# Conditioning panels multiplied in fp32 on four 32-column groups, and four of them at the end of the dense layer

## The reference

```python
def adaln(cond, w, b):
    m = jnp.matmul(jax.nn.silu(cond), w) + b
    return jnp.split(m, 3, axis=-1)

def modulated_norm(x, g, shift, scale):
    return rms_norm_2(x, g) * (1 + scale) + shift
```

## Time and profile before

| what | value |
|---|---|
| median of three runs | 2424.51 us |
| the profiled execution's own time | 2424.6 us |
| its span | 2422.5 us |
| TensorE busy in the span | 2317.7 us (96%) |
| VectorE busy | 1770.3 us (73%) |
| ScalarE busy | 1387.8 us (57%) |
| panel loads | 496 of 1024 KB |
| conditioning panels | 24, from 249.7 to 549.7 us |

### The profile page before, as it was taken

How to read it: one execution, slowest core, us unless ns; L and a number is a source line. 1 busy time by engine, 2 the same in 40 slices (tenths; PEclk the granted TensorE clock), 3 DMA queues, 4 the chain that set the end, 5 groups by cost and what they waited for, 6 DMA issues and landing times. The chain is left out here.

```text
span 2422.5 us, 34387 instructions
## 1 busy us (share of the span) xinstructions
PE 2317.7 (96%) x13625; PEld 2002.4 (83%) x13639; DVE 1770.3 (73%) x1687; ACT 1387.8 (57%) x1382; POOL 20.2 (1%) x42
## 2 busy tenths in 40 slices
PE   7998999999998899999999999999989999899998
PEld 7898999999888788888888888888866885778887
DVE  6765655658764689888988898889877667546773
ACT  6464545447463577777777777777764322744442
POOL 0000000000000000000000000000001000000010
PEclk9999999999999899999999999999999999999999
DMA  6233566654333399989998999899980220025400
GB/s 258 105 140 141 202 249 239 248 207 176 105 140 123 141 373 359 375 333 374 358 375 341 367 366 366 341 368 364 367 336 35 78 97 18 1 71 113 113 1 18
DMA packets 81797, 531.80 MB, mean 220 GB/s; under 512 B 16935, under 2 KB 17224, under 8 KB 17480
## 3 DMA queue, kind: packets, MB, share of 16 engines
q1 hardware_dynamic: 81528, 528.95, 58.8%
q10 hardware_dynamic: 144, 1.05, 0.1%
HBM read 528.91 MB, written 1.05 MB: 219 GB/s over the span
## 5 line engine op out<-in xcount | busy, mean ns | idle before, releaser
L2389 DVE TENSOR_TENSOR ring_low<-ring,M_high 128x2048 fp32r<-128x2048 f32 x336 | 760.9, 2289 | 105.7 <-ACT M_high L1356 99.1
L1356 ACT ACTIVATE M_high<-ring 128x2048 fp32r<-128x2048 f32 x336 | 633.2, 1911 | 4.6 <-DMA ring<-panels 4.0
L485 PE MATMUL ps<-M_high,xe_parts 128*128 128x512 f32 x1344 | 449.2, 397 | 0.0
L485 PEld LDWEIGHTS ps<-M_high,xe_parts 128*128 128x128 f32 x1344 | 252.7, 188 | 51.8
L485 PE MATMUL ps<-ring_low,xe_parts 128*128 128x512 f32 x672 | 262.2, 390 | 0.0
L2261 DVE TENSOR_TENSOR W_low<-ring,W_high 128x2048 fp32r<-128x2048 f32 x66 | 150.2, 2291 | 108.4 <-ACT W_high L1356 108.4
L485 PE MATMUL ps<-h_parts,ring_low 128*128 128x256 f32 x704 | 201.3, 286 | 0.0
L485 PE MATMUL ps<-h_parts,B_high 128*128 128x256 f32 x1024 | 188.6, 286 | 3.6 <-DVE ring_low L2040 1.9
L1356 ACT ACTIVATE W_high<-ring 128x2048 fp32r<-128x2048 f32 x66 | 124.9, 1909 | 97.3 <-PE ps L485 97.3
L485 PE MATMUL ps<-M_high,hid_high 128*128 128x512 f32 x448 | 175.9, 393 | 2.1 <-DVE hid_low L2395 2.1
L485 PE MATMUL ps<-M_high,hid_low 128*128 128x512 f32 x448 | 174.4, 389 | 0.0
(11 more groups left out here) (302 smaller groups left out, 4818.5 us busy)
## 6 DMA issues: line engine op xcount, KB each, us to landing
ring<-panels SPq DMA_DIRECT2D x496, 1024.0 KB, 4.8
arena<-rpb SPq DMA_DIRECT2D x32, 64.0 KB, 8.4
cst<-consts SPq DMA_DIRECT2D x1, 1632.0 KB, 11.9
xT<-x SPq DMA_DIRECT2D x1, 1024.0 KB, 4.9
cT<-ctx SPq DMA_DIRECT2D x1, 1024.0 KB, 7.8
arena<-dft SPq DMA_DIRECT2D x1, 1024.0 KB, 14.4
y<-xT ACTq DMA_DIRECT2D x1, 1024.0 KB, 5.8
proj<-w SPq DMA_DIRECT2D x1, 512.0 KB, 6.1
```

What stands on the lines that cost most here:

```text
L485: return nc.tensor.matmul(o, w, m, start=start, stop=stop, skip_group_check=skip)
L1356: return nc.scalar.activation(o, i, fn, **kw)
L2389: V.tensor_tensor(wide_low(q, 0, PW), ring[:, (q % RING) * PW:(q % RING + 1) * PW], moe_high(q, 0, PW).bitcast(F32), ALU.subtract).then_in ...
```

## The change

Conditioning panels are no longer split. TensorE multiplies them in fp32 straight from the ring: the eight row blocks go in turn to four groups of 32 columns of the array, so that blocks k and k + 4 add up in partitions 32 (k % 4) of the bank. The weights are 32 columns wide (`cond_wide`: the two vectors, and 30 columns of zeros), so all 128 partitions of the bank are written. ScalarE copies all 128 rows, and the turn is a matmul against `cond_pick` (a 128 x 32 matrix with ones where row and column agree modulo 32, of which two columns are used), which also adds up the four partial sums. Split buffers are now counted by dense panels alone (`SPLIT_AT`, `RANK`), and the first splits wait for less. Conditioning pairs stand in steps 2 to 10; four panels are left for the place behind down 13, the last pair in bank 1; two turns come behind the first projection panel.

```diff
-    _pair = 2 <= _f < ADA
+    _pair = 2 <= _f < ADA - 1
...
-DENSE += [("down", FSTEP - 1), ("cond", 2 * ADA - 2), ("cond", 2 * ADA - 1)]
+DENSE += [("down", FSTEP - 1)] + [("cond", 2 * ADA - 4 + _n) for _n in range(4)]
+LAST_CONDS = 4
+SPLIT_AT = [_i for _i, (_kind, _) in enumerate(DENSE) if _kind != "cond"]
+RANK = {_i: _s for _s, _i in enumerate(SPLIT_AT)}
...
-            return arena[0:4, 8704 + (j % 2) * 512:9216 + (j % 2) * 512]
+            return arena[:, 8704 + (j % 2) * 512:9216 + (j % 2) * 512]
+        def ada_bank(j):
+            return 1 if j == ADA - 1 else 2
+        cond_wide = arena[:, 8192:8448]
+        cond_pick = arena[:, 8448:8480]
...
                 def conditioning(p, n):
-                    o = bank(2)[0:4, (n % 2) * S:(n % 2 + 1) * S]
+                    landed(p)
                     for k in range(KD):
-                        high, low = W(p, k * S, (k + 1) * S)
-                        mm(o, cond_parts[:, 4 * k:4 * k + 4], high, k == 0, False)
-                        last = mm(o, cond_parts[:, 4 * k:4 * k + 4], low, False, k == KD - 1)
+                        g = 32 * (k % 4)
+                        last = mm(bank(ada_bank(n // 2))[g:g + 32, (n % 2) * S:(n % 2 + 1) * S],
+                                  cond_wide[:, 32 * k:32 * k + 32], slot(p, k * S, (k + 1) * S), k < 4, k >= 4)
                     last.then_inc(DONE, 1)
                 def conditioning_turn(j):
                     pe.wait_ge(sem("ada_rows_copied"), j + 1)
                     for c in range(4):
-                        last = nc.tensor.transpose(bank(3)[:, (4 * j + c) * 4:(4 * j + c) * 4 + 4],
-                                                   ada_rows(j)[:, c * P:(c + 1) * P], cst[0:4, K_ID:K_ID + 4])
+                        last = mm(bank(3)[:, (4 * j + c) * 2:(4 * j + c) * 2 + 2], ada_rows(j)[:, c * P:(c + 1) * P],
+                                  cond_pick[:, 0:2], True, True)
                     last.then_inc(sem("ada_turned"), 1)
...
-                def last_pair():
-                    for i in (len(DENSE) - 2, len(DENSE) - 1):
-                        pe.wait_ge(sem("panel_split"), i + 1)
-                        if i == len(DENSE) - 2:
-                            pe.wait_ge(sem("ada_rows_copied"), ADA - 1)
+                def last_conds():
+                    pe.wait_ge(sem("ada_rows_copied"), ADA - 2)
+                    for i in range(len(DENSE) - LAST_CONDS, len(DENSE)):
                         conditioning(p0 + i, DENSE[i][1])
+                def last_turns():
+                    conditioning_turn(ADA - 2)
+                    conditioning_turn(ADA - 1)
...
-                for i, (kind, n) in enumerate(DENSE[:-2]):
-                    p = p0 + i
-                    pe.wait_ge(sem("panel_split"), i + 1)
+                for i, (kind, n) in enumerate(DENSE[:-LAST_CONDS]):
+                    if kind != "cond":
+                        q = RANK[i]
+                        pe.wait_ge(sem("panel_split"), q + 1)
...
-                        elif 2 <= n <= ADA:
+                        elif 2 <= n < ADA:
                             conditioning_turn(n - 2)
...
                 if layer:
+                    act.wait_ge(DONE, p0 - 2)
+                    conditioning_rows(ADA - 2)
                     act.wait_ge(DONE, p0)
                     conditioning_rows(ADA - 1)
...
-            def high_part(p, before, rounds):
-                act.wait_ge(LANDED[p % RING], rounds * 16 + 16 * (p // RING + 1))
-                act.wait_ge(DONE, before + (p - 2))
-                f(split(W_high, p, 0, PW), ring[:, (p % RING) * PW:(p % RING + 1) * PW], ACT.Copy) \
+            def high_part(p0, q):
+                p = p0 + SPLIT_AT[q]
+                act.wait_ge(LANDED[p % RING], 16 * (p // RING + 1))
+                act.wait_ge(DONE, p0 + SPLIT_AT[q - SPLIT] + 1 if q >= SPLIT else p0 - 2)
+                f(split(W_high, q, 0, PW), ring[:, (p % RING) * PW:(p % RING + 1) * PW], ACT.Copy) \
                     .then_inc(sem("panel_high"), 1)
...
-                f(ada_rows(j), bank(2)[0:4, :], ACT.Copy).then_inc(sem("ada_rows_copied"), 1)
+                f(ada_rows(j), bank(ada_bank(j)), ACT.Copy).then_inc(sem("ada_rows_copied"), 1)
...
-                for i in range(3, len(DENSE)):
-                    multiplied_panel(i - 3)
-                    if i > 3:
-                        high_part(p0 + i, 0, 0)
-                multiplied_panel(len(DENSE) - 3)
+                seen_to = 0
+                for q in range(2, len(SPLIT_AT)):
+                    if q >= SPLIT:
+                        for i in range(seen_to, SPLIT_AT[q - SPLIT] + 1):
+                            multiplied_panel(i)
+                        seen_to = SPLIT_AT[q - SPLIT] + 1
+                    high_part(p0, q)
+                for i in range(seen_to, len(DENSE) - LAST_CONDS):
+                    multiplied_panel(i)
...
-                    step(f(cond[:, :], sml[:, S_COND:S_COND + 16], ACT.Silu))
-                    f(cond_k[:, :, 0, :], cond[:, :].rearrange("p (k s) -> p k s", s=2), ACT.Copy) \
-                        .then_inc(sem("cond_high"), 1)
+                    f(cond[:, :], sml[:, S_COND:S_COND + 16], ACT.Silu).then_inc(sem("cond_activated"), 1)
...
-                    if layer == 0 and j == 2:
-                        high_part(panel[0], 0, 0)
-                        high_part(panel[0] + 1, -1, 0)
-                    elif layer == 0 and j == 3:
-                        high_part(panel[0] + 2, -2, 0)
+                    if layer == 0 and j == 3:
+                        high_part(panel[0], 0)
                     square_pair(j)
                 norm_root(S, MEAN_BANK[1])
                 if layer == 0:
-                    high_part(panel[0] + 3, 0, 0)
+                    high_part(panel[0], 1)
...
-                    if layer == 0 and j >= 2:
-                        for i in ((0,), (1, 2))[j - 2]:
-                            low_part(p0 + 2 * OUTP + i, i + 1)
+                    if layer == 0 and j == 3:
+                        low_part(p0 + 2 * OUTP, 0)
...
-            def condition_low():
-                dve.wait_ge(sem("cond_high"), 1)
-                V.tensor_tensor(cond_k[:, :, 1, :], cond[:, :].rearrange("p (k s) -> p k s", s=2),
-                                cond_k[:, :, 0, :].bitcast(F32), ALU.subtract).then_inc(sem("cond_split"), 1)
+            def condition_laid():
+                dve.wait_ge(sem("cond_activated"), 1)
+                step(V.memset(cond_wide, 0.0))
+                V.tensor_copy(cond_wide.rearrange("p (k n) -> p k n", k=KD)[:, :, 0:2],
+                              cond[:, :].rearrange("p (k s) -> p k s", s=2))
+                V.tensor_reduce(cond_pick, K(K_ID).rearrange("p (j n) -> p n j", j=4), AX.X, ALU.add) \
+                    .then_inc(sem("cond_laid"), 1)
...
-                    v = bank(3)[:, 96 * layer:96 * layer + 96].rearrange("p (c a s) -> p a c s", a=2, s=2)
+                    v = bank(3)[:, 48 * layer:48 * layer + 48].rearrange("p (c s) -> p c s", s=2)
...
-                    step(V.tensor_tensor(o, o, v[:, 1, :, :], ALU.add))
```

More of the change, by code:

```diff
@@ L783, in dense_layer, with up @@
             def dense_layer(p0):
-                def up(p, b):
+                def up(q, b):
                     for m in range(2):
                         for k in range(KD):
-                            last = mm3(bank(b)[:, m * S:(m + 1) * S], W(p, k * 256 + m * P, k * 256 + (m + 1) * P),
+                            last = mm3(bank(b)[:, m * S:(m + 1) * S], W(q, k * 256 + m * P, k * 256 + (m + 1) * P),
                                        (h_high[:, k * S:(k + 1) * S], h_low[:, k * S:(k + 1) * S]),
@@ L791, in up, with down @@
                     last.then_inc(DONE, 1)
-                def down(p, f):
+                def down(q, f):
                     for k in range(2):
@@ L820, in first_gate @@
                         for m in range(2):
-                            last = mm3(bank(0)[:, m * S:(m + 1) * S], W(p, k * 256 + m * P, k * 256 + (m + 1) * P),
+                            last = mm3(bank(0)[:, m * S:(m + 1) * S], W(q, k * 256 + m * P, k * 256 + (m + 1) * P),
                                        (h_high[:, k * S:(k + 1) * S], h_low[:, k * S:(k + 1) * S]),
@@ L844, in dense_layer @@
                             pe.wait_ge(sem("hidden_made"), n)
-                        up(p, 1)
+                        up(q, 1)
                         if n == 0:
@@ L853, in dense_layer @@
                         if n == 0:
-                            pe.wait_ge(sem("cond_split"), 1)
+                            pe.wait_ge(sem("cond_laid"), 1)
                         elif n % 2 == 0:
                             pe.wait_ge(sem("ada_rows_copied"), n // 2)
-                        conditioning(p, n)
+                        conditioning(p0 + i, n)
                     else:
                         pe.wait_ge(sem("hidden_split"), n + 1)
-                        down(p, n)
```

(26 more changed lines are left out.)

25 lines of the change are left out of this document (12 added, 13 removed).

## The result

Four executions of the changed kernel have a median of 2408.11 us (2406.38 to 2410.49), the four of the kernel before beside them 2424.03 us (2421.69 to 2425.79): a ratio of 0.994, 95% interval 0.9925 to 0.9954, faster by 15.9 us. The forecast was 2413.5 us, range 2410 to 2421. The profiled execution took 2410.49 us.

A forecast was written before the change was run, and what follows sets the result against it. The prediction took TensorE's own instructions to bound the dense layer; its six terms summed to -11.05 us from about 2424.5 us, giving 2413.5 us, with a range of 2410 to 2421 us.

The forecast's parts named there:

- Term 1: Conditioning panels inside the dense layer: 18 at 1.25 us replace 20 at 1.81 us, -13.8 us.
- found inside rows 5: Per-panel overhead of 0.21 us, taken from the earlier trace's stick-breaking output on two 64-column groups.
- Term 2: Turns inside the dense layer: 10 at 0.89 us replace 11 at 0.52 us, +3.2 us.
- Terms 3 and 4: Dense layer's entry, first split no longer waiting for a panel, -0.9 us; kernel's start, one ScalarE copy fewer, -0.25 us.
- Term 5: Dense layer's end: next layer's first panel loads later, delaying the squares, +0.3 us, up to +1.4.
- Term 6: Behind the dense layer: both last turns run past the low part TensorE waits for, +0.4 us.
- Behind 557 us the order is as before, all moves as a whole.: After the dense layer: waits hang on projections that move as a whole; no further gain or loss counted.
- A: Conditioning panels: no more than two streams at once, 2433 us, or 2440 in program order; chance 0.13.
- B: Conditioning panels: streams run one after the other, 3.86 us a panel, 2470 us; chance 0.03.
- C: Conditioning panels: three of four streams at once, 2420 us; chance 0.07.
- D: Gain in the layer comes but is eaten around it, 2417 us; upper edge of the forecast's 0.77 band.
- Signs: Right: layer 10 to 11 us shorter, starts in fours; wrong: paired starts, TensorE waits, half clock behind 252 us, late squares.

The follow-up runs named there:

- two_groups: The changed kernel with a panel's eight matmuls alternating between two 32-column groups instead of four; 2428.73 us, ratio 1.0022 to the kernel before.
- one_group: The changed kernel with all eight matmuls of a panel on one 32-column group, one after the other; 2468.75 us, ratio 1.0187 to the kernel before.
- entry_held: The changed kernel with ScalarE's split of the first up panel waiting until the second conditioning panel is multiplied; 2411.69 us, ratio 0.9957 to the kernel before.
- old_places: The changed kernel's matmuls and turns at the old places: 20 panels and 11 turns inside the dense layer; 2411.88 us, ratio 0.9951 to the kernel before.
- pairs: The changed kernel with each pair's two conditioning panels one behind the other, behind gate f; 2405.29 us, ratio 0.9924 to the kernel before.
- before_again: The kernel before, unaltered, run once more for a second trace; 2424.93 us, ratio 1.0005.
- again: The changed kernel, unaltered, run once more; 2408.92 us, ratio 0.9936 to the kernel before.
- adjacent: The changed kernel with a panel's matmuls in group order 0 0 1 1 2 2 3 3 instead of 0 1 2 3 0 1 2 3; 2408.67 us, ratio 0.9944 to the kernel before.

## Why the prediction was right, and where it fell short

- **Bound.** Right: only TensorE's instructions counted inside the layer; VectorE's and ScalarE's saved work was worth nothing there.
- **Term 1, panels.** Mechanism right, size off: 1.191 us against 1.25, so 18 x 1.191 - 20 x 1.814 = -14.8 instead of -13.8. The streams are 0.86 as taken, and so are the borders: the first instruction starts 0.21 us behind the last dense one instead of 0.12, and the second dense matmul 0.22 us behind the first. What was too large is the 0.21 "found inside rows 5": from the panel's first start to the next dense matmul are 1.00 us, so 0.14 on top of the streams (0.12 in two_groups and in one_group). It was taken over from a product of another shape; why that one has more is not shown.
- **Term 2, turns.** 0.893 us against 0.89, and 0.526 before: 10 x 0.893 - 11 x 0.526 = +3.1. The sum is right by two errors that cancel: the turn's second instruction starts 0.03 us behind its first instead of 0.11, and the second dense matmul behind it comes 0.08 us late, though no shape changes.
- **Terms 3 and 4, entry and start.** -1.36 us together in the means of four, against -1.15. The entry's part is 0.92 us in every trace (1.54 against 2.46), and entry_held shows its cause. The start has 0.33 (16.87 against 17.20, each kernel's four traces within 0.06 us), but old_places and pairs, whose start is that of the changed kernel, have 17.16 and 17.15: that the missing copy is the cause isn't shown. The half clock that might follow the idle time, 1.95 us in all four traces of the changed kernel, came in one of them:

```profile
255.10:258.50 3.40, 3.40 (x17) 3.40 (x17) 3.40 (x11) 2.03 (x5) 0.00 (x0) 0.50 1.01 424
```

  It made that layer's stretch 0.15 us longer (274.33 against 274.18 in the other three): the first up panel's wait covers it, as said.
- **Term 5, the late load.** The squares start 0.96, 1.43, 1.64 and 1.02 us behind VectorE's sum, before always 0.72: +0.5 on average, forecast +0.3 and up to +1.4. ScalarE's split of the next layer's first panel stands in front of them, and it waits for the load.
- **Term 6, last turns.** Project 1's second panel comes 7.54 us behind its first, against 7.07: +0.47, forecast +0.4.
- **Sum at that point.** -11.05 forecast, -12.1 in the means of four traces. Until here the miss is 1.1 us, term 1's.
- **"Behind 557 us the order is as before, all moves as a whole."** This is the step that failed, beside term 1's size. The order on TensorE is as before, but ScalarE's instructions are 49 fewer, and its last DMA issue no longer stalls: 5.96 us from TensorE's last matmul to the end instead of 8.24, so -2.3 us, which the sum put at nothing. No term looked at how many instructions an engine executes, only at how long they take. Term 1 and this step together, -3.4 us, are more than the 1.9 us by which the result lies below the range.
- **The rest.** 1.2 us behind the layer remain in the means of four traces, and 1.17 of them stand in the router's part (15.66 and 14.49 us). Whether that is chance or comes with the change is open, as said there. Over 57 executions of before (45 beside the experiments, 12 of before_again) and 9 of the changed kernel (the first four and again's), the means are 2424.2 and 2408.4: -15.8, with an interval of about 1.3 to either side. The sum of what is shown, -12.1 and -2.3, is -14.4; the remaining 1.4 us are about that interval, and in the traces most of them stand in the router's part.
- **Rivals.** A, B and C are refuted by the starts and by one_group and two_groups; D (the gain eaten around the layer) has 1 us in it (the fourth row of the table) and was met by more on the other side. The range failed at its lower end, because it was closed 0.15 us of overhead a panel below the forecast, and every unknown outside the layer was counted as a loss or as nothing.
- **Signs.** The panels in fours and the turns came as announced, and 1.19 us a panel lies just below the 1.2 to 1.3. The layer is 11.8 us shorter, not 10 to 11. Two signs of "wrong" showed as well: the half clock behind 252 us in one trace, and squares of the second layer over 1 us behind VectorE's sum in three of four (1.43, 1.64, 1.02). They cost 0.15 and some 0.5 us, so they weren't signs against the mechanism.

## What to carry to other kernels

A matmul with few output columns can run four at a time on column groups at the full factor, in both orders of issue that were tried; what it costs is the stop, so put several small products into one stop. When a change takes instructions from an engine or adds some, look at how long the kernel's last DMA issue takes and which instruction packets come with it: here this was worth 2 us, and a few idle instructions moved it. Hold several traces of either kernel side by side before a difference far from the change is put down to it or to chance. Give the range room for what has no term.

## What the runs showed of the hardware that was not expected

- Four 32-column groups stream fp32 at once without loss: 3.76, 2.04 and 1.19 us a panel with one, two and four.
- An instruction of an idle column group starts ahead of waiting ones, up to twelve places in front (adjacent: four starts within 0.04 us).
- A stop of fp32 panels on four groups in the dense fp32r stream costs 0.33 us beyond its streams, whether one panel or two stand in it.
- ScalarE's last DMA issue lasted 2.2 to 2.5 us in the five traces where instruction packets started 0.7 to 1.0 us into it, and 0.38 or 0.39 in the 13 others; 49 idle instructions far ahead of it brought the stall back, 24 took it away.
- The same router instructions take from 14.2 to 16.2 us in unaltered kernels by the clock granted in that execution (0.76 and 0.63 in the mean).
